# Softmax attentions with rows normalised by VectorE and GpSimd before they are turned, and values in two matmul passes

## The reference, cut to what matters

```python
z = jnp.einsum("bhqd,bshd->bhqs", q_blk, k).astype(jnp.float32) * scale
...
p = jax.nn.softmax(jnp.where(allowed, z, -jnp.inf), axis=-1)
return jnp.einsum("bhqs,bshd->bhqd", p.astype(v.dtype), v)
```

## Time and profile before

| | us |
|---|---|
| median of three runs | 1711.18 (1711.05 to 1711.73) |
| the profiled execution | 1711.5 |
| its span in the trace | 1709.7 |
| PE busy | 1688.6 (99%) |
| DVE busy | 1272.5 (74%) |
| ACT busy | 957.2 (56%) |
| POOL busy | 169.8 (10%) |
| mla attention in the trace | 299.7 to 383.9 |
| fox attention in the trace | 515.8 to 682.0 |

### The profile page before, as it was taken

How to read it: one execution, slowest core, us unless ns; L and a number is a source line. 1 busy time by engine, 2 the same in 40 slices (tenths; PEclk the granted TensorE clock), 3 DMA queues, 4 the chain that set the end, 5 groups by cost and what they waited for, 6 DMA issues and landing times.

```text
span 1709.7 us, 25289 instructions
## 1 busy us (share of the span) xinstructions
PE 1688.6 (99%) x9375; PEld 1459.4 (85%) x9375; DVE 1272.5 (74%) x2020; ACT 957.2 (56%) x1645; POOL 169.8 (10%) x147
## 2 busy tenths in 40 slices
PE   9999999999999999999999999999999999999998
PEld 7888877888788897789899988878887999999977
DVE  6378877776567776589698986775566978898966
ACT  4267875665436666478556364652235866464655
POOL 2011212000300000220000002320003000000041
PEclk9999999999999999999999999999999999999999
DMA  8222124214243222243232433313322432323621
GB/s 270 84 73 74 40 73 101 75 50 148 75 110 76 74 75 81 74 173 117 81 121 81 145 152 132 99 62 103 114 91 87 161 123 99 99 99 100 234 75 50
DMA packets 152786, 177.52 MB, mean 104 GB/s; under 512 B 18281, under 2 KB 126342, under 8 KB 150886
## 3 DMA queue, kind: packets, MB, share of 16 engines
q1 hardware_dynamic: 150790, 159.22, 29.8%
q10 hardware_dynamic: 1888, 16.85, 2.5%
HBM read 158.82 MB, written 12.58 MB: 100 GB/s over the span
## 4 chain that ended last, share of the span: by engine, by line
PE 88%; DVE 8%; ACT 3%; issue 1%; DMA 1%; DVEq 0%; SPq 0%; ACTq 0%
PE bank L1158 27%; PE bank L1159 26%; PE bank L1160 26%; PE bank L1507 2%; DVE split_weights L2671 2%; PE bank L1531 1%; PE bank L1426 1%; DVE act_b L2671 1%; PE bank L1415 1%; DMA raw_weights<-in_w_mlp_down 1%; DVE act_a L2673 0%; PE bank L1823 0%; ACT act_a L1920 0%; DVE work L2706 0%; PE bank L1341 0%
## 5 line engine op out<-in xcount | busy, mean ns | idle before, releaser
L1158 PE MATMUL bank<-act_a,split_weights 128*128 128x512 f32 (+1 forms) x1360 | 525.4, 386 | 6.3 <-DVE act_a L2671 2.0
L1160 PE MATMUL bank<-act_a,split_weights 128*128 128x512 f32 (+1 forms) x1360 | 518.8, 381 | 0.0
L1159 PE MATMUL bank<-act_a,split_weights 128*128 128x512 f32 (+1 forms) x1360 | 518.1, 381 | 0.0
L1158 PEld LDWEIGHTS bank<-act_a,split_weights 128*128 128x128 f32 x1360 | 256.0, 188 | 58.5 <-issue 6.1
L1160 PEld LDWEIGHTS bank<-act_a,split_weights 128*128 128x128 f32 x1360 | 255.6, 188 | 50.3
L1159 PEld LDWEIGHTS bank<-act_a,split_weights 128*128 128x128 f32 x1360 | 256.0, 188 | 45.1 <-issue 0.2
L1158 PE MATMUL bank<-act_b,split_weights 128*128 128x256 f32 (+1 forms) x648 | 207.4, 320 | 0.3 <-DVE split_weights L3355 0.2
L1160 PE MATMUL bank<-act_b,split_weights 128*128 128x256 f32 (+1 forms) x648 | 206.4, 318 | 0.0
L1159 PE MATMUL bank<-act_b,split_weights 128*128 128x256 f32 (+1 forms) x648 | 206.3, 318 | 0.0
L2613 DVE TENSOR_TENSOR split_weights<-raw_weights,split_weights 128x2048 fp32r<-128x2048 f32 x55 | 127.1, 2311 | 76.1 <-ACT split_weights L1865 63.3
L1865 ACT ACTIVATE split_weights<-raw_weights 128x2048 fp32r<-128x2048 f32 x51 | 97.3, 1908 | 119.5 <-PE bank L1160 119.5
(11 more groups left out here) (356 smaller groups left out, 3261.5 us busy)
## 6 DMA issues: line engine op xcount, KB each, us to landing
raw_weights<-in_w_mlp_up SPq DMA_DIRECT2D x32, 1024.0 KB, 5.4
raw_weights<-in_w_mlp_down SPq DMA_DIRECT2D x32, 1024.0 KB, 5.3
raw_weights<-in_w_in SPq DMA_DIRECT2D x18, 1024.0 KB, 5.3
raw_weights<-in_w_conv_in SPq DMA_DIRECT2D x12, 1024.0 KB, 5.2
raw_weights<-in_w_attn_in SPq DMA_DIRECT2D x16, 512.0 KB, 5.3
raw_weights<-in_w_ple_gate SPq DMA_DIRECT2D x8, 1024.0 KB, 5.1
raw_weights<-in_w_out SPq DMA_DIRECT2D x4, 1024.0 KB, 5.1
raw_weights<-in_w_attn_in SPq DMA_DIRECT2D x4, 1024.0 KB, 5.4
```

The lines of the kernel that those rows point to most:

```text
L1158: nc.tensor.matmul(dst, w[0], a[0], start=first, stop=False)
L1159: nc.tensor.matmul(dst, w[0], a[1], start=False, stop=False)
L1160: mm = nc.tensor.matmul(dst, w[1], a[0], start=False, stop=last)
```

## The change

What was one wait between `exp` and turn becomes a chain over three engines, the inverse after the values goes, and the values take two passes:

- `e` (ACT) also gives the sum of each of its rows into `row_sums[:, s]` by its accumulator.
- A new step n s (DVE) waits for `exp` of row s and inverts the 128 sums in place.
- POOL runs a new stream `normed_rows`: for each row, in order, it waits for n s and multiplies `tmp[:, s % 4]`, 128 x (j+1)*128 elements, in place by the inverse. Turns wait for this.
- V's low part takes the place of the ones beside V's high part. The high weights run through both (128 stationary columns), the low weights through V's high part alone (64 columns): 8 matmuls for 12. Rows 64 to 127 of the result are then a second part of the output.
- `r` (ACT) is one copy of these rows for Ln and Exp, and `g` (DVE) adds where it multiplied.
- The two memsets that wrote ones and zeros beside V (L3108) go.

```diff
-        DVE_MLA = "m0 m1 m2 m3 p0 p1 p2 m4 p3 m5 c0 c1 c2 y1 m6 p4 c3 m7 p5 s2 p6 g0 p7 y2 x0 x1 s3 g1"
+        DVE_MLA = "m0 m1 n0 m2 n1 m3 p0 n2 p1 n3 p2 m4 p3 m5 c0 n4 c1 n5 c2 y1 m6 p4 n6 c3 m7 p5 s2 n7 p6 g0 p7 y2 x0 x1 s3 g1"
-        DVE_FOX = "m0 m1 c0 m2 c1 p0 m3 s2 p1 m4 m5 p2 p3 y0 m6 c2 m7 c3 y1 p4 p5 g0 p6 p7 x0 x1 s3 g1"
+        DVE_FOX = "m0 m1 c0 n0 m2 n1 c1 p0 m3 n2 s2 p1 m4 n3 m5 p2 p3 y0 n4 m6 n5 c2 m7 n6 c3 y1 p4 p5 n7 g0 p6 p7 x0 x1 s3 g1"
-        DVE_NEAR = "m0 m1 m2 m3 p0 y0 c0 c1 p1 p2 m4 m5 p3 m6 c2 c3 o0 o1 p4 y1 m7 p5 g0 x0 x1 p6 p7 s2"
+        DVE_NEAR = "m0 n0 m1 n1 m2 m3 p0 y0 c0 n2 c1 p1 n3 p2 m4 m5 p3 n4 m6 n5 c2 n6 c3 o0 o1 p4 y1 m7 p5 n7 g0 x0 x1 p6 p7 s2"
...
                 def turn(i, s):
-                    pe.wait_ge(A["exp"], 8 * i + s + 1)
+                    pe.wait_ge(A["normed"], 8 * i + s + 1)
...
                     for kt in range(TT):
                         c = min(kt * P, S - 2 * P)
-                        three(banks[5][:, c:S], [head_v[:, hh, hl, kt, :] for hl in (0, 1)],
-                              [act_b[:, hl, kt, c:S] for hl in (0, 1)], kt == 0, kt == TT - 1,
-                              A["out"] if kt == TT - 1 else None)
+                        out_, v = banks[5][:, c:S], head_v[:, hh, 0, kt, :]
+                        if kt:
+                            nc.tensor.matmul(out_[0:HD, :], v[:, 0:HD], act_b[:, 1, kt, c:S], start=False, stop=False)
+                        mm = nc.tensor.matmul(out_, v, act_b[:, 0, kt, c:S], start=kt == 0, stop=kt == TT - 1)
...
-                                         bias=negmax[:, s:s + 1]).then_inc(A["exp"], 1)
-                def invert_sums(i, hh):
-                    h = 2 * i + hh
-                    act.wait_ge(A["out"], FREE + h + 1)
-                    nc.scalar.activation(sum_inverse(hh), banks[5][HD:2 * HD, :], ACT.Ln).then_inc(A["sum_log"], 1)
-                    act.wait_ge(A["sum_log"], h + 1)
-                    nc.scalar.activation(sum_inverse(hh), sum_inverse(hh), ACT.Exp, scale=-1.0).then_inc(A["sum_inverse"], 1)
+                                         bias=negmax[:, s:s + 1], accum_out=row_sums[:, s:s + 1]).then_inc(A["exp"], 1)
+                def parts_out(i, hh):
+                    act.wait_ge(A["out"], FREE + 2 * i + hh + 1)
+                    nc.scalar.activation(low_rows(hh), banks[5][HD:2 * HD, :], ACT.Copy).then_inc(A["parts_copied"], 1)
...
-                    dve.wait_ge(A["sum_inverse"], 2 * i + hh + 1)
-                    V.tensor_tensor(dst, src, sum_inverse(hh), ALU.mult).then_inc(A["gathered"], 1)
+                    dve.wait_ge(A["parts_copied"], 2 * i + hh + 1)
+                    V.tensor_tensor(dst, src, low_rows(hh), ALU.add).then_inc(A["gathered"], 1)
...
+                def inverse(i, s):
+                    dve.wait_ge(A["exp"], 8 * i + s + 1)
+                    V.reciprocal(row_sums[:, s:s + 1], row_sums[:, s:s + 1]).then_inc(A["sum_inverse"], 1)
...
+            def normed_rows(kind, pairs):
+                A = ATT[kind]
+                for i in range(pairs):
+                    for s in range(2 * TT):
+                        part = tmp[:, s % 4, 0:(s % TT + 1) * P]
+                        pool.wait_ge(A["sum_inverse"], 8 * i + s + 1)
+                        nc.gpsimd.tensor_scalar(part, part, row_sums[:, s:s + 1], None, ALU.mult).then_inc(A["normed"], 1)
```

## The result

| | before | after |
|---|---|---|
| median, us | 1711.12 (1710.29 to 1711.73) | 1778.97 (1777.09 to 1780.63, 4 runs) |
| span of the profiled execution, us | 1709.7 | 1778.6 |

The ratio is 1.0397, with a 95% interval of 1.0379 to 1.0415: the change costs 67.9 us, in the direction that was forecast and nearly twice the forecast 35.8; the time lies above the range.

A forecast was written before the change was run, and what follows sets the result against it. PE bounds the kernel, so new waits at turns are lost: 4 mla pairs x 3.9, 6 fox pairs x 3.2 and +1 give +35.8 on 1711.5, 1747 us, after 15.5 saved by the passes; range 1728 to 1772.

The forecast's parts named there:

- What bounds the kernel: PE, busy 1688.6 of 1709.7 us; every new wait in its stream is lost, with 0.25 us to spare at fox t7.
- The passes: Values products on PE: two passes for three save 0.65 us a head, 15.5 us over 24 heads.
- the term for POOL's multiply: Between reciprocal and turn: 0.40, 0.55, 0.75 and 0.95 us for 128, 256, 384 and 512 columns.
- The prediction's own recurrence: Step-by-step walk of a pair's turns with the priced links, giving +3.2 us a fox pair and +3.9 an mla pair.
- POOL held up by DVE: Rival: multiplies slowed beside DVE's two-operand instructions, 10 pairs x 1.0 us more; 1762 us with somewhat dearer multiplies; chance 0.22.
- The small prices: Links besides the multiply: accumulator read 0.12, reciprocal 0.10, steps to DVE 0.03, POOL 0.08 and PE 0.05 us.
- t0: First turn of a pair: its delay paid for by the shorter r, about 0.5 us at the pair's head; counted as nothing.
- L: How late PE is against before at each turn: fox 1.46 us at t1 to 3.82 at t7; mla 4.54 at t7.
- Pairs: Whole attention pairs after the passes' saving: +3.2 us for each of six fox pairs, +3.9 for each of four mla pairs.
- NEAR and LAST: The two last fox pairs, where projections between scores and turns leave room: put at +1 and 0 us.
- What would show it: PE busy below 85% in mla, idle ended by POOL, fox pairs about 24 us, mla 24.9, 192 new POOL instructions.

The follow-up runs named there:

- experiment 2: Changed kernel, weights not normalised: multiply left out, turns waiting for reciprocal 1716.88 us; turns waiting for exp 1702.65 us; multiply of first 128 columns only 1751.31 us.
- experiment 5: Changed kernel with spare transposes ahead of the waits of four fox turns, and the wait for an earlier row's low part moved ahead: 1779.21 us.
- experiment 6: Changed kernel with orders rewritten so turns stand later: usual fox pairs 1736.79 us, plus mla 1712.81, plus last two fox pairs 1704.78; kernel before in these orders 1721.18.

## Why the prediction was right, and where it was wrong

- **What bounds the kernel: right.** Time taken out of PE's stream is won, and the slack from `exp` to turn is too small for the links. The sign follows: even the link without any multiply (experiment 2, 1716.9 us) costs more than the passes save.
- **The passes: nearly right.** 1.28 us a head for 1.29 forecast; 13.1 us of the 15.5 show when nothing else is changed.
- **The step that failed is the term for POOL's multiply.** The prediction put 0.40, 0.55, 0.75 and 0.95 us, between DVE's rate and POOL's additions of two tiles; measured alone it is 0.60, 0.92, 1.24 and 1.56. The upper bound, 1.29 for 512 columns, was no bound: it rested on one input less having to be cheaper, which no row showed. The rule of the Trainium skill that was weighed beside it (GPSIMD Engine Reference, section 4.1, "Engine selection": one-input elementwise work at roughly line rate) pointed further down still; here the measurement decides against it, 1.56 us on POOL for what DVE does in 0.49. How much of the miss this is, is an estimate, not a measurement. The prediction's own recurrence, walked through all steps of several pairs, gives for 4 mla and 6 fox pairs +33 us with the forecast prices, and +51 with only the four multiplies set right: 18 of the 32 us that were missing. Experiment 2 gives nearly the same: the forecast had 45% too little for the columns beyond 128, which measured 27.7 us, and 0.20 of 0.98 us too little for the multiply of 128 columns with its two steps, which measured 34.4; together 20.
- **POOL held up by DVE** was put down as a rival and not into the sum. It is there beside c1 (+0.36), s2 (+0.51 for 384 columns) and c2, and is another 5 us in the recurrence. It alone did not decide; taking one such collision away gave its 0.36 us back in a pair at the same clock, which the median of the whole kernel does not resolve.
- **The small prices** nearly cancel: the accumulator about 0.10 for 0.12, the reciprocal 0.157 for 0.10, the steps to POOL and PE 0.09 and 0.06 for 0.08 and 0.05. 3 us in the recurrence, which then stands at +59 for the 61 us by which these ten pairs grew.
- **t0 was not free.** n0 stands behind c0 on DVE; t0 comes 0.81 us late behind m0 in the fox pair shown and 0.66 late in mla, more than the 0.5 that the shorter `r` was to pay.
- **L, step by step, in the fox pair shown** (from m0, against the pair of the earlier trace rows): 2.60, 3.83, 4.06, 4.97, 6.25 and 7.39 at t1, t2, t3, t4, t5 and t7, for 1.46, 1.65, 1.91, 2.64, 3.39 and 3.82. The places were right, the sizes not, t1 and t2 above all. t7 in mla: 6.49 for 4.54.
- **Pairs:** the six usual fox pairs last 165.7 us for 123.9 before, +6.96 each for 3.2 forecast (+6.0 to +6.8 in the three with the full clock throughout); mla pairs +4.2 to +5.3 for 3.9. NEAR and LAST, put at +1 and 0, took 5.0 and 1.7 more: their projections did not cover the waits, of which the longest are 2.2 us at t2 of NEAR and 1.6 at t1 of LAST.
- **The clock** was in no term. Some fox pairs are longer for it, but experiment 5 puts that at some 3 us.
- **What would show it:** PE's busy share of mla 81% (below 85% forecast), its idle time ended by POOL at the turnings, and the long ones at t1, t5 and t7 of fox and t3, t6 and t7 of mla, but also at t2 and t4 of fox and at t1 and t4 of mla. POOL has 96 new instructions; the 192 of the prediction was a miscount (24 heads of 4 rows).
- **What the forecast didn't ask:** whether the orders could be written anew. The loss is one of latency, so it went away with room (experiment 6).

## What to carry to other kernels

A link that is added between two steps of a software pipeline costs its latency wherever the order leaves less slack than that, whatever the load of the engine that does it: price it at each place from measured rows of the same operation on the same engine, and when no such row exists, do not cap the price by a neighbour with "more" work. If the links are dear but the bound engine gets shorter, first rewrite the order so that each consumer stands a link's length later behind independent work, and only then judge the change. A single wait that is taken away is won, but a few tenths of a us in a pair drown in the scatter of the whole: judge it by pairs that ran at the same clock, and for a gain move all the waits.

## What the hardware showed that was not expected

- GpSimd's multiply of one f32 tile by a scalar took 0.28 us + 2.5 ns a column (0.60 to 1.56 us for 128 to 512 columns), 0.07 less with a constant; its addition of two tiles took 1.29 for 512. VectorE's same multiply took 0.29 to 0.49.
- Beside VectorE instructions that read two SBUF operands the multiply grew from 0.92 to 1.28 (256 columns) and from 1.24 to 1.75 or 2.25 (384), while VectorE mostly kept its own length. Beside the 384 columns of t2 it is one or the other: in two fox pairs the multiply took 1.75 us and VectorE's second instruction of s2 0.98 for 0.68, in others the multiply took 2.25 and VectorE 0.68.
- Waits of 0.7 to 1.6 us, several in a pair, were followed by pieces of 3.4 us at 1.2 GHz in three of the six usual fox pairs and not in the other three, nor in mla after waits of 0.9 to 1.5 us. With the waits filled the granted clock stayed at 2.4 GHz in fox and the median of the whole kernel did not change.
